# Per-head centring moved from the recurrence's output to its values, and the rotary turn done by eight transfers

## The reference

```
state = state * w_t + sa (x) b_t + v_t (x) k_t ;  y_t = state r_t      # per head
mu  = mean(y, over the head's 64)
var = mean((y - mu)^2)
y   = (y - mu) * rsqrt(var + 64e-5)
```

```
out = concat(t1*cos - t2*sin, t2*cos + t1*sin)
```

## Time and profile before

| | |
|---|---|
| time, median of 3 runs | 1403.31 us (1403.28 to 1404.31) |
| the profiled execution | 1401.52 us, its span 1400.2 us |
| PE busy | 1382.5 us, 99% of the span |
| DVE, ACT, POOL busy | 812.5, 479.2, 128.5 us |
| PE's granted clock | 0.999 of full speed |

### The profile page before, as it was taken

One profiled execution on the slowest core, in us unless ns is written; L12 is line 12 of the kernel. 1 busy time (PEld: TensorE's weight loads), 2 busy tenths in 40 slices (PEclk: granted clock), 3 DMA queues, 4 the chain that ended last, 5 costly groups with the idle time before them and its releaser, 6 DMA issues.

```text
span 1400.2 us, 20877 instructions
## 1 busy us (share of the span) xinstructions
PE 1382.5 (99%) x8982; PEld 1104.5 (79%) x8982; DVE 812.5 (58%) x1142; ACT 479.2 (34%) x723; POOL 128.5 (9%) x134
## 2 busy tenths in 40 slices
PE   7999999999999999999999999999999999999998
PEld 5687887878778888887788888887887877888886
DVE  7375655656558645455575774555636335776654
ACT  6332324234244343233432221323243233444323
POOL 1020302002002010001210000000040012000000
PEclk9999999999999999999999999999999999999999
DMA  5110202011052333222255442222221223211352
GB/s 191 59 46 32 79 30 75 33 47 62 32 180 91 106 125 119 88 76 78 95 193 190 181 170 100 91 98 94 87 95 71 102 96 112 82 61 61 102 169 90
DMA packets 42204, 136.15 MB, mean 97 GB/s; under 512 B 4649, under 2 KB 8361, under 8 KB 42112
## 3 DMA queue, kind: packets, MB, share of 16 engines
q1 hardware_dynamic: 33984, 114.57, 24.0%
q0 software_dynamic: 4080, 14.65, 2.8%
q10 hardware_dynamic: 4048, 5.59, 1.1%
HBM read 130.34 MB, written 2.10 MB: 95 GB/s over the span
## 4 chain that ended last, share of the span: by engine, by line
PE 96%; DVE 3%; ACT 1%; DMA 0%; issue 0%; ACTq 0%; DVEq 0%
PE bank L418 94%; PE bank L421 2%; DVE w_lo L1425 0%; DVE opA_lo L1433 0%; DVE tmp L1433 0%; DMA xT<-x 0%; ACT scores L935 0%; DVE P L1433 0%; DVE scores L1433 0%; DVE stat L1970 0%; DVE scores L1425 0%; ACT opA_hi L935 0%; DVE x_tokens L1433 0%; ACT w_hi L935 0%; DVE tmp L1425 0%
## 5 line engine op out<-in xcount | busy, mean ns | idle before, releaser
L1425 DVE TENSOR_TENSOR w_lo<-w_raw,w_hi 128x1024 fp32r<-128x1024 f32 (+1 forms) x209 | 256.7, 1228 | 351.0 <-ACT w_hi L935 350.8
L418 PE MATMUL bank<-opA_hi,w_hi 128*128 128x512 f32 x1000 | 410.9, 411 | 10.0 <-DVE opA_lo L1433 7.9
L418 PE MATMUL bank<-opA_hi,w_lo 128*128 128x512 f32 x1000 | 396.0, 396 | 0.0
L418 PE MATMUL bank<-opA_lo,w_hi 128*128 128x512 f32 x1000 | 394.7, 396 | 0.0
L935 ACT ACTIVATE w_hi<-w_raw 128x1024 fp32r<-128x1024 f32 (+1 forms) x209 | 220.1, 1053 | 366.0 <-DMA w_raw<-panels 365.7
L418 PEld LDWEIGHTS bank<-opA_hi,w_hi 128*128 128x128 f32 x1000 | 188.3, 188 | 63.8 <-issue 15.7
L418 PEld LDWEIGHTS bank<-opA_hi,w_lo 128*128 128x128 f32 x1000 | 188.3, 188 | 45.4
L418 PEld LDWEIGHTS bank<-opA_lo,w_hi 128*128 128x128 f32 x1000 | 188.4, 189 | 42.2 <-issue 2.2
L418 PE MATMUL bank<-opB_hi,w_hi 128*128 128x512 f32 x448 | 178.4, 398 | 0.3 <-DVE w_lo L1425 0.3
L418 PE MATMUL bank<-opB_hi,w_lo 128*128 128x512 f32 x448 | 177.2, 395 | 0.0
L418 PE MATMUL bank<-opB_lo,w_hi 128*128 128x512 f32 x448 | 177.2, 395 | 0.0
(11 more groups left out here) (316 smaller groups left out, 1607.2 us busy)
## 6 DMA issues: line engine op xcount, KB each, us to landing
w_raw<-panels SPq DMA_DIRECT2D x208, 512.0 KB, 3.3
ada_w<-ada POOLq DMA_DIRECT2D x24, 512.0 KB, 4.4
xT<-x ACTq DMA_DIRECT2D x1, 2048.0 KB, 14.3
x_tokens<-x_blocks SPq DMA_DIRECT2D x16, 128.0 KB, 4.0
out<-x_tokens SPq DMA_DIRECT2D x8, 256.0 KB, 2.0
memT<-mem ACTq DMA_DIRECT2D x1, 1024.0 KB, 5.7
xT<-x ACTq DMA_DIRECT2D x3, 256.0 KB, 7.4
xT<-x SPq DMA_DIRECT2D x3, 256.0 KB, 7.3
```

Of the source, the lines that this page charges most:

```text
L418: return pe.matmul(o, lhsT, rhs, start=start, stop=stop, skip_group_check=True)
L1425: return ve.tensor_tensor(o, a, b, op)
```

## The change

For the recurrence: DVE sums `UV[64:128]` over each head's 64 values, in two instructions per f (rounds n = 1 and 2 of the solve, behind the panel step and ahead of the additions to `X`). POOL multiplies the 8 sums of each with -1/64 and adds them back onto the 64 x 512 values. PE's product `UV,GT` waits for that (`v_centred`) in place of `uv_done`. At the end of f PE's `head_sum` product of `y` and DVE's subtraction are gone; DVE squares `y` directly.

For the rotary turn: the `rotate` matrix and its five products are gone. At the start of panel `ub`, POOL issues eight transfers from SBUF to SBUF, which put each half of 32 partitions of K and of the four Q tiles in the other half's place: four of 64 KB (K) and four of 256 KB (Q). The sign goes into the sine table, by way of the frequencies (`inv_freq`, negative for the first half). DVE's product with the sine now reads the swapped tile in SBUF and writes it in place.

```diff
 MATS = [... 
-        ("rotate", 128), ("causal", 128), ("eye", 64), ("level1_turned", 64)] + [...]
+        ("causal", 128), ("eye", 64), ("level1_turned", 64)] + [...]
+    v_mean = cols[64:128, 24:24 + 2 * NC]
-    rot = [place(f"rotated{n}", [NP, S], scores_at + n * TB) for n in range(2)]
+    rot_q = place("rotated_q", [NP, 4, S], r_opB)
+    rot_k = place("rotated_k", [NP, S], r_opB + 8 * TB)
+    rot = [rot_k[:, :]] + [rot_q[:, t, :] for t in range(4)]
# PE, recurrence
             p.steps(F_Z)
-            pe.wait_ge(uv_done, 2 * f + 2)
+            pe.wait_ge(v_centred, 2 * f + 2)
...
-            p.steps(1)
-            pe.wait_ge(y1_done, f + 1)
-            mm(bank[2][:, :], mat("head_sum"), y[:, :]).then_inc(ysum_mm, 1)
-            p.steps(F_TAIL)
-            pe.wait_ge(yc_done, 2 * f + 2)
+            p.steps(1 + F_TAIL)
+            pe.wait_ge(ysq_done, f + 1)
             head_columns(ysq, bank[3])
# PE, second block
-        def rotate(n, t):
-            if 2 <= n < 4:
-                pe.wait_ge(rope_sin, n - 1)
-            mm(bank[ROPE_BANKS[n]][:, :], mat("rotate"), P[:, t, :]).then_inc(rot_mm, 1)
-
-        p.multiply()
-        for i in range(FIRST["ub"] - 2, FIRST["ub"]):
-            pe.wait_ge(left[i % 2], left_after(i))
-        rotate(0, K2)
-        rotate(1, Q2)
-        p.leave()
         p.to("zb")
         p.multiply()
         pe.wait_ge(vb_made, 4)
-        for t in range(1, 4):
-            rotate(1 + t, Q2 + t)
+        for i in range(FIRST["ub"] - 2, FIRST["ub"]):
+            pe.wait_ge(left[i % 2], left_after(i))
# POOL, recurrence, behind XT
+            for r in range(2):
+                s = v_mean[:, NC * r:NC * r + NC]
+                gp.wait_ge(v_sums, 2 * f + r + 1)
+                gp.tensor_scalar(s, s, -1.0 / HD, None, ALU.mult).then_inc(v_means, 1)
+                gp.wait_ge(v_means, 2 * f + r + 1)
+                v = UV[64:128, 4 * r:4 * r + 4, :].rearrange("p c (h v) -> p (c h) v", h=2)
+                tt(v, v, s.unsqueeze(2).broadcast_to([64, NC, HD]), ALU.add).then_inc(v_centred, 1)
# POOL, second block
+        p.to("ub")
+        for i in range(FIRST["ub"] - 3, FIRST["ub"] - 1):
+            gp.wait_ge(left[i % 2], left_after(i))
+        for a in range(0, NP, HD):
+            b, c = a + HD // 2, a + HD
+            for d, s in ((slice(a, b), slice(b, c)), (slice(b, c), slice(a, b))):
+                load(halves_here, rot_k[d, :], P[s, K2, :])
+                load(halves_here, rot_q[d, :, :], P[s, Q2:Q2 + 4, :])
...
         def rope(n, dst, t):
-            gp.wait_ge(rot_mm, n + 1)
             if n == 0:
+                gp.wait_ge(halves_here, 8 * 16)
                 gp.wait_ge(trig_done, 2)
             tt(dst, P[:, t, :], cosT[:, :], ALU.mult).then_inc(rope_pool, 1)
# DVE, a round of the solve
                 p.steps(F_SOLVE)
+                if n in (1, 2):
+                    r = n - 1
+                    ve.wait_ge(uv_done, 2 * f + r + 1)
+                    ve.reduce_sum(v_mean[:, NC * r:NC * r + NC],
+                                  UV[64:128, 4 * r:4 * r + 4, :].rearrange("p c (h v) -> p (c h) v", h=2),
+                                  AX.X).then_inc(v_sums, 1)
# DVE, end of f
-            ve.wait_ge(ysum_mm, f + 1)
-            stt(y[:, :], bank[2][:, :], -1.0 / HD, y[:, :], ALU.mult, ALU.add).then_inc(yc_done, 1)
-            ve.wait_ge(yc_done, 2 * f + 1)
-            tt(ysq[:, :], y[:, :], y[:, :], ALU.mult).then_inc(yc_done, 1)
+            ve.wait_ge(y1_done, f + 1)
+            tt(ysq[:, :], y[:, :], y[:, :], ALU.mult).then_inc(ysq_done, 1)
# DVE, second block
         def rope(n, dst):
-            ve.wait_ge(rot_mm, n + 1)
+            ve.wait_ge(halves_here, 8 * 16)
             ve.wait_ge(trig_done, 2)
-            tt(rot[n % 2][:, :], bank[ROPE_BANKS[n]][:, :], sinT[:, :], ALU.mult).then_inc(rope_sin, 1)
+            tt(rot[n], rot[n], sinT[:, :], ALU.mult).then_inc(rope_sin, 1)
             ve.wait_ge(rope_sin, n + 1)
             ve.wait_ge(rope_pool, n + 1)
-            tt(dst, dst, rot[n % 2][:, :], ALU.add).then_inc(rope_done, 1)
+            tt(dst, dst, rot[n], ALU.add).then_inc(rope_done, 1)
# host
-        "inv_freq": np.tile(freq, 4),
+        "inv_freq": np.concatenate([-freq, freq, -freq, freq]),
```

More of the change, by code:

```diff
@@ L48 @@
 MATS = [("ident", 128), ("mean", 128), ("head_sum", 128), ("cumsum", 128), ("chunk_mask", 128),
-        ("rotate", 128), ("causal", 128), ("eye", 64), ("level1_turned", 64)] + [(f"level{s}", 64) for s in LEVELS[:-1]]
+        ("causal", 128), ("eye", 64), ("level1_turned", 64)] + [(f"level{s}", 64) for s in LEVELS[:-1]]
 MAT = {}
@@ L67, in constants @@
         "chunk_mask": np.where(j < 64, (i % 64) < (j % 64), (i % 64) <= (j % 64)),
-        "rotate": np.where((j % 64) < 32, -1.0 * (i == j + 32), 1.0 * (i == j - 32)),
         "causal": i <= j,
@@ L121 @@
 TOKEN_BANKS = ((4, 5), (6, 7), *((j, 2 + j) for j in (FIRST["out2"] % 2, 1 - FIRST["out2"] % 2)))
-ROPE_BANKS, V2_BANK = (6, 7, 6, 7, 2), 3
+V2_BANK = 3
 F2_LAST = 16 * KT - 2 - 4 * (F2_MAX + F2_SOFTMAX + F2_OUT)
@@ L387, in build @@
                                                     sem("output_multiplied"))
-    y1_done, ysum_mm, yc_done, y6_done, y7_done, yg_done = (
-        sem("y_out"), sem("y_summed"), sem("y_centred_and_squared"), sem("y_normed"), sem("y_affine"),
-        sem("y_bonus_and_gated"))
+    y1_done, ysq_done, y6_done, y7_done, yg_done = (
+        sem("y_out"), sem("y_squared"), sem("y_normed"), sem("y_affine"), sem("y_bonus_and_gated"))
+    v_sums, v_means, v_centred = sem("v_sums_by_head"), sem("v_means"), sem("v_centred")
     merge_sum = sem("merge_summed")
@@ L401, in build @@
         sem("token_spread"), sem("x4_scaled"))
-    angle_step, trig_done, rot_mm, rope_pool, rope_sin, rope_done = (
-        sem("angle_step"), sem("sine"), sem("rotated"), sem("rope_cosine"), sem("rope_sine"), sem("rope_made"))
+    angle_step, trig_done, halves_here, rope_pool, rope_sin, rope_done = (
+        sem("angle_step"), sem("sine"), sem("swapped_halves_here"), sem("rope_cosine"), sem("rope_sine"), sem("rope_made"))
     vb_made = sem("gating_values_made")
```

## The result

The changed kernel takes 1395.58 us (median of 5 runs, 1393.98 to 1397.94) against 1403.33 us (5 runs, 1403.28 to 1404.31): the ratio is 0.9945, 95% interval 0.9933 to 0.9956, so 6.2 to 9.4 us less. The forecast was 1395.5 us.

What follows compares the result with a forecast made beforehand. PE was taken to bound the kernel, busy 99% of the span. Products removed save 3.7 + 4.3 = 8.0 us, sums give back 0.2, all else nothing: 1403.3 - 7.8 = 1395.5 us, range 1394.4 to 1398.4.

Steps and rivals of the forecast that it cites:

- The products: On PE, four `y` products at the ends of f save 3.7 us, five `rotate` products in the turn 4.3 us.
- The sums: Eight DVE sums in the solves, 0.69 us each; 0.1 us lost in each of two places, 0.2 us together.
- POOL's centring: Eight small and eight large POOL instructions ahead of PE's `UV,GT`; costed at nothing, with over 6 us of cover.
- POOL beside DVE: POOL's two-input work stretches nothing behind the solves' sums; the turn's five sine products could take 1.7 us instead of 0.7.
- The transfers: Eight transfers at panel `ub`, 5.9 us of engine time beside two panel loads; taken at nothing, with 5.6 us of cover.
- the prediction's own sign: Sign of being right: `w_hi` of the two panels near 1088 us lands within 3 us of its old place.
- upper end: Worst case for the transfers at `ub`: 5.9 us of delay and some 2 us more, about 2.5 us lost.
- The sum: Whole kernel: 8.0 us saved on PE less 0.2 us for the sums, 7.8 us less, so 1395.5 us.
- rival 1: DVE becomes the bound of the solve: 1396.7 us with a sum of 1.4 us, up to 1400.8; chance 0.08.
- Rival 3: The transfers delay a panel's weights near `ub`: 2.5 us lost, 1398.0 us; chance 0.04.
- Rival 2: POOL's centring meets `w_lo` in the solves and stretches it: up to 3.2 us lost, 1398.7 us; chance 0.03.
- Rivals 4 and 5: 4: PE waits before `UV,GT` for centred values, 1406 us (chance 0.02); 5: no gain, PE awaits weights, 1403 us (chance 0.01).

Runs made afterwards that it cites:

- e1: The changed kernel with only the recurrence's part of the change, the rotary turn as in the kernel before; 1399.64 us, ratio 0.9972 to the kernel before.
- e2: The changed kernel with only the rotary turn's part of the change, the recurrence as in the kernel before; 1398.58 us, ratio 0.9968 to the kernel before.
- e4: The changed kernel with every sum over UV made twice on DVE, the second into spare columns; 1397.57 us, ratio 0.996 to the kernel before.
- e5: The changed kernel with each of the eight transfers issued twice, the second time into free space; 1398.86 us, ratio 0.9979 to the kernel before.
- e6: The changed kernel with transfers moved to `vb` and sums moved to solve rounds where DVE idles; 1396.15 us, ratio 0.9947 to the kernel before.
- e3: The changed kernel with the eight transfers issued one stage later, in `vb`; 1395.52 us, ratio 0.9944 to the kernel before.

## Why the prediction was right, and where it was off

**The products.** Forecast 3.7 and 4.3 us; the account shows 3.64 and 4.29, e1 and e2 the same each by itself. Costing a matmul by the distance between the panel matmuls around it, and not by its busy time, carried to a twentieth of a microsecond. The rows of before gave 590 ns and more for each of two halves of such a product, which would have made 1.2 us of each.

**The sums.** Forecast 0.69 us each and 0.1 lost in each of two places. Measured 0.68 and 0.18 and 0.14. The line of DVE, with POOL's product, from the view of lines by form, beside the earlier trace rows:

```profile
L1271 POOL TENSOR_TENSOR UV<-UV,cols 64x512 f32<-64x512 f32 x8 | 8.3, 1042 | 0.7
L1718 DVE TENSOR_REDUCE cols<-UV 64x8 f32<-64x512 f32 x8 | 5.5, 682 | 0.2
```

What passes the slack is in DVE's timeline in f = 3, n = 2, beside the earlier trace rows:

```profile
349.95 1.22 DVE L1428 TENSOR_TENSOR w_lo<-w_raw,w_hi 128x1024 fp32r<-128x1024 f32 x1
351.20 0.68 DVE L1718 TENSOR_REDUCE cols<-UV 64x8 f32<-64x512 f32 x1
351.91 0.75 DVE L1428 TENSOR_TENSOR X<-X,bank 128x256 f32<-128x256 f32 x2
```

Before, `X` started 0.05 us ahead of the end of `w_lo`; here the sum starts 0.03 us behind that end, and `X` 0.03 us behind the sum's. Measured from PE's product `Y,XT` of the round, `X` started 0.73 us behind it before (352.92 to 353.65). Here `Y,XT` starts at 350.39, so `X` would start at 351.12; it starts at 351.91. The sum has put 0.79 us there and not 0.69. The Trainium skill states such a hold: by "VectorE: DVE Perf Modes", section "Two Vector instructions with no wait between them", an instruction whose data begin in another quarter of the partitions than those of the one before starts only when all before it have ended. The sum begins at partition 64 and its neighbours at 0; the trace agrees, with 0.03 us behind in place of 0.05 to 0.09 ahead.

**POOL's centring.** Costed at nothing, and it is: 0.23 + 1.04 us, ended at 353.3 in f = 3, where PE comes at 360.1.

**POOL beside DVE.** The prediction watched the sine products; the five took 0.68 us each, as POOL was computing nothing then. It placed POOL's cosine products at about 1095 and 1145 us and did not ask which `w_lo` they would meet there, as the earlier trace rows would have let it. They meet two. The first is the one of the step at 1104 (1.70 us here, 2.19 in e4, where it cost 0.23 us). The second, beside three cosine products (POOL, 1142.32, 3.81 us), took nearly three times its 1.23 us:

```profile
1143.67 3.56 DVE L1428 TENSOR_TENSOR w_lo<-w_raw,w_hi 128x1024 fp32r<-128x1024 f32 x1 [0.82 <-ACT w_hi L923]
```

PE was not late for it: the account stays at -3.40 from 1144 to 1160 us.

**The transfers.** This is the step that was off: taken at nothing, with the cover read from `w_lo` of the panel in flight, 5.6 us. Their engine time was right (6.2 against 5.9 us), and that first panel was early enough. Wrong was which load suffers and what stands behind it. The load issued behind the transfers landed when nearly all of them had, 4.8 us late against before (`w_hi` at 1096.84, where 1094.43 less 2.4 was its old place), so the prediction's own sign, both panels within 3 us of their old place, failed for the second. What PE then waited for stands behind that panel's `w_hi` in two chains: the bank that ACT empties, and `w_lo` beside POOL. In the changed kernel's two traces they ended within 0.2 us of each other; in e5 the bank came last by 0.65 us, in e4 `w_lo` by 0.31. By the rows of before this could have been seen: `w_hi` at 1094.43, a table load, the emptying at 1096.8, PE's need at 1101.7, so some 4 us to spare behind a load that was 3.7 us on its way, about 8 us in all, where the runs show 7.8. The cost, 0.4 to 0.7 us here and 0 to 1.1 over all executions, lay inside the 2.5 us that the prediction kept as upper end.

**The sum.** By the steps that belong to it, the change gives 7.93 us less 0.32 and 0.70, that is 6.9 us in the first pair of traces, where 7.8 were forecast. The medians differ by 7.75 us, closer to the forecast than the steps are. The 0.9 us between lie within what scatters from execution to execution (the ratio's interval is 6.2 to 9.4 us), so that the forecast time was met to 0.1 us is in part luck. Two small slips in the prediction's numbers change nothing: 0.9 us below the forecast is 1394.6, where the range starts at 1394.4, and 1395.5 less 0.2 and plus 1.3 is 1396.6, where rival 1 has 1396.7.

**The rivals.** Rival 1 is refuted at this size of the sum and confirmed as a mechanism by e4. Rival 3 is what happened, at 0.43 and 0.70 us of its 2.5, by another load than the one it named. Rival 2 is refuted for the centring: `w_lo` keeps its 1.22 us in the solves; POOL's cosine products are what stretched one. Rivals 4 and 5 are refuted by `UV,GT` that waits for nothing, and by the account, in which every step that PE won is still there at the end.

## What to carry to other kernels

Where one engine sets the time, cost a piece of its work by the distance between its neighbours' starts, and afterwards set the two streams side by side and read the steps: a change of 0.5% then splits into terms of 0.1 us that no median resolves. Work put on another engine between two of its steps costs what exceeds idle time plus slack, so put it in the rounds where that engine idles. The burst of transfers here harmed the load that was issued behind it and not the one in flight; ask what is queued behind that load's first reader, not only when the loaded data are needed. And where work on POOL is set free from one wait, look up what it will run beside next.

## What the runs showed of the hardware

Behind 32 matmuls of a single column each, PE's granted clock averaged 1.00 or 0.65 over the next few microseconds, in two executions of before and in two of the changed kernel, and 0.53 in e6, whose instructions at this place are the same. The stretch took 3.87, 4.89 and 5.85 us. Between the two executions of the changed kernel this place makes 0.95 of the 1.0 us by which their spans differ, between the two of before 0.95 of 1.3; the wider scatter of e5 (1397.0 to 1402.8 us) was not profiled. In e5 the clock fell too, to the lower of the two levels (1.2 and 2.4 GHz; granted clock 0.50, starts 0.43 us apart and not 0.23), behind a wait of 2.77 us, while the 0.45 us wait in the changed kernel and the 0.80 us wait in e4 were followed by no fall.

Beside three of POOL's two-input products, DVE's `w_lo` of 128 x 1024 took 3.56 us and not 1.23. A load of 512 KB issued by SP just behind eight transfers of POOL's (1.3 MB from SBUF to SBUF, 6.2 us of all 16 engines) was 7.5 to 8.6 us on its way in four traces; in the traces of before, e1, e3 and e6, with no transfers at that place, it was 3.7 to 4.4 us.
